# Order of the gathered v rows and u rows in the expert stage of a hybrid encoder step

## The reference, cut to what matters

```python
def one_block(args):
    xb, ib, gb = args                                   # 128 tokens, their 128 picks, the gates
    u = jnp.take(u_tab, ib, axis=0)
    h = jax.nn.gelu(jnp.einsum('nkd,nd->nk', u, xb), approximate=False)
    vv = jnp.take(v_tab, ib, axis=0)
    return jnp.einsum('nk,nkd->nd', gb * h, vv)
```

## Time and profile before

| what | us |
|---|---|
| median of three executions | 5407.66 |
| the profiled execution | 5398.55 |
| its span in the trace | 5396.8 |
| PE busy in the span | 4784.7 (89%) |
| DVE busy | 3049.7 (57%) |
| POOL busy | 2328.4 (43%) |
| ACT busy | 1391.7 (26%) |

### The profile page before, as it was taken

The page is one execution under the profiler, slowest core; times in us unless marked ns, Lnnn a source line. Parts: engine busy times, 40 slices in busy tenths (PEclk is TensorE's granted clock), DMA queues, the critical chain, the costliest instruction groups (busy, mean ns, idle before and its releaser), DMA issues. The chain is left out here.

```text
span 5396.8 us, 90990 instructions
## 1 busy us (share of the span) xinstructions
PE 4784.7 (89%) x35388; PEld 4604.9 (85%) x35388; DVE 3049.7 (57%) x4962; ACT 1391.7 (26%) x1809; POOL 2328.4 (43%) x892
## 2 busy tenths in 40 slices
PE   6999888888898889969788667999999999999998
PEld 5999877777888789969778667999999999999997
DVE  4333244444444422249978555577776777767775
ACT  3333211222121121121233222222222222222222
POOL 3222211211121133332322233577777777777773
PEclk8999999999999999989889888899999999999999
DMA  6999623333322245732224677677777777777773
GB/s 239 337 335 337 206 71 103 103 97 103 96 83 76 64 157 191 247 114 69 82 114 176 236 246 257 244 272 258 268 261 254 271 258 269 262 257 268 260 270 122
DMA packets 327119, 1070.22 MB, mean 198 GB/s; under 512 B 97552, under 2 KB 130832, under 8 KB 245776
## 3 DMA queue, kind: packets, MB, share of 16 engines
q1 hardware_dynamic: 275136, 776.20, 43.2%
q0 software_dynamic: 36864, 268.45, 12.8%
q10 hardware_dynamic: 14928, 22.84, 1.1%
HBM read 873.50 MB, written 193.88 MB: 198 GB/s over the span
## 5 line engine op out<-in xcount | busy, mean ns | idle before, releaser
L154 POOL TENSOR_TENSOR wlo<-raw,whi 128x2048 fp32r<-128x2048 f32 x156 | 717.8, 4603 | 2249.2 <-ACT whi L150 2249.2
L168 POOL TENSOR_TENSOR wlo<-raw,whi 128x1024 fp32r<-128x1024 f32 x460 | 1111.9, 2418 | 662.4 <-ACT whi L164 658.9
L164 ACT ACTIVATE whi<-raw 128x1024 fp32r<-128x1024 f32 x460 | 487.2, 1060 | 1217.7 <-PE psR L236 721.1
L2086 DVE TENSOR_TENSOR H<-psR,H 128x416 f32<-128x416 f32 x832 | 487.0, 590 | 431.2 <-PE psR L236 431.2
L236 PE MATMUL accs<-xh,whi 128*128 128x272 f32 x2624 | 580.7, 303 | 69.5 <-DMA at_before<-in_cst 40.5
L236 PE MATMUL psR<-chi,whi 128*128 128x416 f32 x1664 | 590.3, 355 | 54.8 <-DVE H L2086 54.8
L236 PE MATMUL psS<-hh,wlo 128*128 128x416 f32 x1664 | 588.0, 353 | 0.0
L236 PE MATMUL psR<-chi,wlo 128*128 128x416 f32 x1664 | 587.4, 353 | 0.0
L236 PE MATMUL psS<-hh,whi 128*128 128x416 f32 x1664 | 585.2, 352 | 0.2 <-DVE clo L2075 0.2
L236 PE MATMUL psS<-hl,whi 128*128 128x416 f32 x1664 | 582.9, 350 | 0.0
L236 PE MATMUL psR<-clo,whi 128*128 128x416 f32 x1664 | 582.7, 350 | 0.0
(11 more groups left out here) (378 smaller groups left out, 8868.6 us busy)
## 6 DMA issues: line engine op xcount, KB each, us to landing
raw<-in_u SPq DMA_DIRECT2D x128, 1024.0 KB, 5.1
raw<-in_v SPq DMA_DIRECT2D x128, 1024.0 KB, 5.9
raw<-in_w_in SPq DMA_DIRECT2D x82, 1024.0 KB, 7.3
at_UI<-in_u SPq DMA_DIRECT2D x64, 1024.0 KB, 8.9
u_d<-at_UO SPq DMA_DIRECT2D x256, 256.0 KB, 6.2
g_d<-STG SPq DMA_DIRECT2D x8, 3328.0 KB, 10.3
Ge<-g_d SPq DMA_DIRECT2D x64, 416.0 KB, 8.4
rw_UI<-in_u SPq DMA_DIRECT2D x48, 512.0 KB, 5.5
```

The lines of the kernel that those rows point to most:

```text
L154: pool.tensor_tensor(self.lo[:, c % 2, :], self.raw[:, c % 2, :], self.hi[:, c % 2, :].bitcast(F32), ALU.subtract).then_inc(self.split_don ...
L164: act.activation(self.half(self.hi, c, h), self.half(self.raw, c, h), ACT.Copy).then_inc(self.hi_done, 1)
L168: pool.tensor_tensor(self.half(self.lo, c, h), self.half(self.raw, c, h), self.half(self.hi, c, h).bitcast(F32), ALU.subtract).then_inc(se ...
L2086: dve.tensor_tensor(h, v_bank(d, per), h, ALU.add).then_inc(S["ex_added"], 1)
```

## The change

In each phase the v rows now come first and the u rows after them; the list of gathers has the same order, ScalarE's wait for the dot products is moved to the new end of the u rows, and the index of the row in `HD` follows. Nothing else is altered: phases have as many rows of each kind as before, and the waits for coefficients name the same phases.

```diff
@@ experts: the phases
-            gathers += [("u", dotted + n) for n in range(nu)] + [("v", summed + n) for n in range(nv)]
+            gathers += [("v", summed + n) for n in range(nv)] + [("u", dotted + n) for n in range(nu)]
@@ gather_gelu
-                s, n, _, _, at = phases[j]
+                s, n, _, nv, at = phases[j]
                 if n:
-                    act.wait_ge(S["gx_done"], GBUF + at + n)
+                    act.wait_ge(S["gx_done"], GBUF + at + nv + n)
@@ rows_of
-                    if m < nu:
+                    if m >= nv:
+                        x = s + m - nv
                         dve.tensor_tensor_reduce(r, r, accs.rearrange("p b n -> p (b n)"), 1.0, 0.0, ALU.mult, ALU.add,
-                                                 HD[:, s + m:s + m + 1]).then_inc(S["gx_done"], 1)
+                                                 HD[:, x:x + 1]).then_inc(S["gx_done"], 1)
                     else:
-                        x = t + m - nu
-                        if m == nu:
+                        x = t + m
+                        if m == 0:
                             dve.wait_ge(S["gx_coef"], 1 + max(p for p in range(j) if phases[p][1] and phases[p][0] <= t + nv - 1))
```

## The result

The changed kernel takes 5416.26 us (median of 11 runs, 5399.95 to 5435.95); the kernel before, run on the same chip, takes 5399.54 (11 runs). The ratio is 1.003, 95% interval 1.0016 to 1.0043: **slower by about 17 us**, where 5400 and no measurable change were forecast. (The 5400 started from 5407.66, the median of three executions; -7 us from 5399.54 would be 5392.) The time lies inside the range, on the side that had a chance of 0.2.

The account below looks back on a forecast made before the run. TensorE waits only for VectorE's adds to `H`, set by when VectorE's last row ends. 24 x (-0.35 - 0.11) = -11, and +4 for phase 1, is -7 us: 5400 us, no measurable change, range 5370 to 5440.

Parts of the forecast that it names:

- The cost at the front: Start of a phase: first v row holds GpSimd's first `wlo` half to 4.47 us; gather 5 starts 2.87 us later.
- I take it to be served behind the load again: load at 5.78, gather at 5.78 + 8.48 = 14.26: Landing of gather 4: issued with SyncE's raw load, it lands behind that load, 8.48 us after 5.78, at z+14.26.
- It lands at 18.16: Landing of gather 5, even phases: 3.9 us behind gather 4, at z+18.16; adds start 0.11 us earlier than before.
- The odd phase: Odd phases: half goes before third v row, gather 5 is locked out, lands at z+18.46; adds 0.35 us earlier.
- rival A: Odd phases: third v row goes before the half, gather 5 lands near z+18.0; -18 us, 5390; chance 0.2.
- Rival B: Landings: gathers do not queue behind the load, gather 4 lands at z+13.06; -29 us, 5379; chance 0.15.
- Rival C: Landing of gather 5: fixed time after its late issue, z+18.96 to 19.66; +24 to +58 us, 5432 to 5466; chance 0.2.
- Phase 1: One-time cost: first v row ahead of `coef_lo` delays TensorE's second u unit 5.4 us; +4 us, between +2 and +7.

Follow-up runs that it names:

- u, v, u: The changed kernel with one u row at the head of each phase, then the v rows, then the other u rows: 5337.71 us.
- `coef_lo` first: The changed kernel with VectorE making `coef_lo` of the second u unit before row 1 of the phase instead of after it: 5378.28 us.

## Why the prediction was wrong

- **The cost at the front: right.** The half takes 4.47 us and gather 5 starts at z+11.18 in even phases (forecast 11.16).
- **"I take it to be served behind the load again: load at 5.78, gather at 5.78 + 8.48 = 14.26": the step that failed.** The load did hold the gather up, but the duration was wrong: 8.48 us was that of a free gather, and this one was locked out for 2.83 us. It took 9.60 us (15.36 less 5.76). The text charged the lock-out to what stood behind gather 4 on GpSimd, not to gather 4 itself. Free gathers that leave with the load keep the old duration: in u, v, u row 4 is there 8.6 us after the issue (4409.10 less 4400.49), and that row is a u row too, so the kind of row is not the reason. That the lock-out made the difference of 1.1 us is argued from this and not shown.
- **"It lands at 18.16", 3.9 us behind gather 4: right as a rule, wrong by its start.** Row 5 started at 19.04, 3.68 behind row 4. So the error of 1.10 us in one landing went through: row 5 came 0.88 us later than forecast, and the first add 0.78 us later than before (z+21.26 against 20.48, means) where a gain of 0.11 was forecast, 24 times.
- **The odd phase: right in the number, not in the way.** The third v row went ahead of the half in all 24 odd phases, which is rival A's order (gather 5 out at z+12.63, A had 12.7). Row 5 started at 18.38 on average, in about half of the phases by the chain behind a row 4 that was 1.1 us late (VectorE waited under 0.1 us for it there), in the others by its landing; the forecast had 18.46 by a late gather 5, A 18.0. The gain, 0.40 us a phase, is the forecast's 0.35 by accident.
- **Rival B** (no queueing behind the load) falls: a smaller load brought row 4 in 2.16 us sooner.
- **Rival C** had the sign, and in 15 even phases nearly its landing (row 5 at z+19.16 to 19.74, C had 18.96 to 19.66). Its mechanism falls: gather 5 with the same issue took 7.86 us beside the full load and 5.58 beside a quarter of it (19.04 less 11.18; 16.77 less 11.19), and in odd phases on average at most 5.75 (18.38 less 12.63). There is no fixed time.
- **The clock: not thought of.** 7.8 of the 17 us. The text took a stall to cost its own length. The kernel before had shown otherwise, once: behind TensorE's stall of 3.74 us in phase 1 the granted clock was 0.50 (first line below), and the 16 adds took 18.37 us from the first start to the last, where regular phases take 16.8.
- **Phase 1: a half-right term.** TensorE's second u unit stalled for 4.69 us (forecast 5.4), but the first v row, which only writes `Y`, took 1.28 us, not 2.34 to 3.48; the adds' stall there shrank from 3.74 to 1.83 us, and the dip of the clock behind it was gone (16.84 us from the first add to the last). Counted from the stage's first `psS` matmul (3409.38 before, 3408.64 after), phase 2 starts 1.5 us later, below the +2 to +7 given.

PE in phase 1 of the kernel before (length, busy time with the matmuls, granted clock); then VectorE's first v row and TensorE's second u unit, in phase 1 of the changed kernel:

```profile
3447.00:3449.00 2.00, 2.00 (x8) 0.50 0.97 315
```

```profile
3431.67 1.28 DVE L2105 TENSOR_SCALAR Y<-R,HD 128x2048 f32<-128x2048 f32 x1 [8.20 <-issue]
...
3433.59 0.71 PE L236 MATMUL psS<-hh,whi 128*128 128x416 f32 x1 [4.69 <-DVE clo L2075]
```

What stays open is the lock-out's share in gather 4's 9.6 us: no experiment separated it, and the kernel before speaks against a fixed price. Its gather of row 1, locked out for 2.83 us and issued beside a raw u load, landed after 7.8 us in odd phases and 9.1 in even ones (means). Nor is it known which of the sixteen parts come late, and why.

In odd phases row 5 comes within 3.0 us of row 4 though its gather goes out later than in even ones (12.63 against 11.18). The packets tell a part of the reason: in odd phases all sixteen parts of gather 5 end between z+17.3 and 18.0 (means), in even ones thirteen end by z+16.3 and three at 17.3, 18.1 and 18.7. The raw u load that goes out at z+14.78 runs beside these in even phases, but it is not enough by itself: with a quarter of the v load it goes out as early, and all sixteen parts are in by z+16.4. That the late parts of gather 5 are held up by those of gather 4 is argued.

## What to carry to other kernels

When an instruction is moved, ask which transfers its neighbour on the shared port sends off, loads as well as gathers, and what leaves at the same time: here 2.1 us on one half of a `wlo` split sent off a load and a gather later, and that cost more than 119 us less busy time on VectorE gave back. A landing time may be carried over only from a transfer that was issued in the same manner (free or locked out, alone or with a load). And before reordering whole kinds of work, try the smallest move: one short row ahead of the long ones gave the whole stall back.

## What the runs showed of the hardware that was not expected

- **Who gets the shared port is not just who starts first.** Where a `wlo` half follows a gather directly, it won against a v row that had started 0.42 us before it (all 24 odd phases of the kernel before) and lost against one that had started 0.73 us before (all odd phases of the changed one). The half that came from idle lost to a v row 0.13 us ahead of it, in every regular phase. The Trainium skill (SBUF — State Buffer, Who interferes with whom) gives the port to whoever issues first; the last two cases agree with that, the first does not.
- **A stall of TensorE can cost more than its length.** 17 regular phases of the changed kernel stalled for over 1.9 us; in five of them (stalls of 2.05 to 2.34 us) the granted clock fell to 0.50 behind the stall and about 1.56 us more was lost. The longest stall, 2.93 us in phase 31, kept its clock of 1.00. No regular phase of the kernel before showed a fall, with stalls of 1.05 and 1.58 us. What tells the five from the other twelve was not found.
- **Gather 4 pays for the plain load that leaves with it, and that load hardly pays for the gather.** The load landed after 5.9 us beside gather 4 (phase 28 of the change) and after 5.7 with the head start of 2.3 us (`coef_lo` first); the gather's landing moved by about 2 us. Other loads did pay: the second raw u load of a phase, which leaves with gather 3, landed after 9.6 us in even and 9.2 in odd phases of the change (the 9.4 of the page), 5.1 before; what held it up was not tried. The Trainium skill (DMA: Bandwidth & Descriptors, SWDGE vs HWDGE vs iDMA) says that a DMA engine goes round between the queues of gathers and plain loads; these runs do not show an even share.
